# A hybrid attention block on one core: the top-k bisection's small instructions and passes, the compression's place in the attention units, and the order of the first step

## The reference, cut to what matters

```python
z = rmsnorm(h, norm_mix) @ w_in                 # one projection, split by columns
# NSA: compressed keys/values, selected blocks, sliding window
blocks = blocks + pos_emb                       # windows of 32 tokens, stride 16
kc = gelu(flat @ w1) @ w2                       # compress_tokens, for k and for v
# DSA: an indexer picks 256 keys for each query
score = einsum('bqh,bqhs->bqs', iw_c, relu(idx_logits))
score = where(key_pos <= t_c, score, NEG_INF)
_, sel = top_k(score, 256)                      # then softmax attention over those keys
y = sigmoid(g_A) * y_A + sigmoid(g_B) * y_B     # merged, projected, then a SwiGLU FFN
```

## Time and profile before

| what | value |
|---|---|
| median of 3 runs | 1703.89 us (1701.45 to 1705.29) |
| profiled execution | 1705.37 us, its span 1703.7 us |
| PE busy | 1611.9 us (95%) |
| DVE busy | 1236.4 us (73%) |
| ACT / POOL busy | 689.7 / 617.8 us (40% / 36%) |
| mean granted clock | 0.987 |

### The profile page before, as it was taken

One profiled execution on the slowest core, in us unless ns is written; L12 is line 12 of the kernel. 1 busy time (PEld: TensorE's weight loads), 2 busy tenths in 40 slices (PEclk: granted clock), 3 DMA queues, 4 the chain that ended last, 5 costly groups with the idle time before them and its releaser, 6 DMA issues.

```text
span 1703.7 us, 25436 instructions
## 1 busy us (share of the span) xinstructions
PE 1611.9 (95%) x9216; PEld 1356.0 (80%) x9216; DVE 1236.4 (73%) x2208; ACT 689.7 (40%) x1383; POOL 617.8 (36%) x440
## 2 busy tenths in 40 slices
PE   5899979999989988999999988999999999999997
PEld 5777777888868877789878877888888888887885
DVE  5778897999944756788776328676776667668978
ACT  5554343321155657666622023423222222343445
POOL 3224223322141124434322024444444443544454
PEclk9999999999999999999999999999999999999999
DMA  5013132633161201001034441234333224374433
GB/s 192 13 50 113 58 101 80 191 99 99 50 161 50 101 26 51 14 14 39 26 124 149 130 142 62 62 105 126 101 116 110 93 93 161 132 268 158 153 112 117
DMA packets 153691, 172.19 MB, mean 101 GB/s; under 512 B 19552, under 2 KB 103520, under 8 KB 153312
## 3 DMA queue, kind: packets, MB, share of 16 engines
q1 hardware_dynamic: 153568, 170.57, 31.5%
HBM read 121.00 MB, written 49.55 MB: 100 GB/s over the span
## 4 chain that ended last, share of the span: by engine, by line
PE 48%; DMA 3%; DVE 3%; issue 1%; POOL 1%; ACT 1%; SPq 0%; DVEq 0%; ACTq 0%
PE psA L1554 9%; PE psA L1556 9%; PE psA L1555 8%; PE psT L1555 5%; PE psT L1556 5%; PE psT L1554 5%; PE psT L1561 2%; DMA wd<-in_w_down_dram 2%; PE psT L1757 2%; PE psA L1646 1%; PE psA L1647 1%; POOL w_lo L396 1%; DVE h L2343 0%; DMA gates<-scratch_gates 0%; DVE h L2359 0%
## 5 line engine op out<-in xcount | busy, mean ns | idle before, releaser
L396 POOL TENSOR_TENSOR w_lo<-w_raw,w_hi 128x1024 fp32r<-128x1024 f32 (+2 forms) x52 | 120.4, 2319 | 249.0 <-ACT w_hi L391 249.0
L1377 ACT ACTIVATE s<-s,nmax 128x640 f32<-128x640 f32 (+7 forms) x192 | 144.0, 752 | 37.7 <-DVE nmax L2214 36.3
L1154 POOL TENSOR_TENSOR w_lo<-w_sum,w_hi 128x1024 fp32r<-128x1024 f32 x44 | 115.6, 2629 | 119.8 <-ACT w_hi L1440 119.8
L1177 POOL TENSOR_TENSOR w_lo<-act_raw,w_hi 128x512 fp32r<-128x512 f32 x77 | 106.9, 1390 | 108.7 <-ACT w_hi L1468 108.7
L1561 PE MATMUL psT<-ident,s 128*128 128x128 f32 x816 | 120.9, 278 | 1.6 <-ACT pT L1387 1.6
L1554 PE MATMUL psA<-w_hi,xTh 128*128 128x512 f32 (+2 forms) x320 | 121.4, 379 | 0.2 <-issue 0.2
L1556 PE MATMUL psA<-w_hi,xTl 128*128 128x512 f32 (+2 forms) x320 | 118.4, 370 | 0.0
L1555 PE MATMUL psA<-w_lo,xTh 128*128 128x512 f32 (+2 forms) x320 | 118.3, 370 | 0.0
L1561 PEld LDWEIGHTS psT<-ident,s 128*128 128x128 f32 x816 | 95.1, 142 | 17.2 <-issue 7.1
L2434 DVE TENSOR_TENSOR w_lo<-wd,w_hi 128x512 fp32r<-128x512 f32 x77 | 89.3, 1163 | 23.8 <-ACT w_hi L1475 23.3
L2303 DVE COPY pT<-psT 128x512 f32<-128x512 f32 (+1 forms) x116 | 69.7, 600 | 49.8 <-PE psT L1561 49.7
(11 more groups left out here) (371 smaller groups left out, 4780.4 us busy)
## 6 DMA issues: line engine op xcount, KB each, us to landing
act_raw<-scratch_act SPq DMA_DIRECT2D x77, 256.0 KB, 3.0
w_raw<-in_w_in_dram SPq DMA_DIRECT2D x28, 512.0 KB, 4.1
scratch_act<-act SPq DMA_DIRECT2D x33, 256.0 KB, 2.1
scratch_act<-act_sum SPq DMA_DIRECT2D x33, 256.0 KB, 2.1
wd<-in_w_down_dram SPq DMA_DIRECT2D x33, 256.0 KB, 3.0
scratch_gates<-gate_out SPq DMA_DIRECT2D x32, 256.0 KB, 2.9
gates<-scratch_gates SPq DMA_DIRECT2D x32, 256.0 KB, 4.3
a<-in_w_gate_dram SPq DMA_DIRECT2D x22, 256.0 KB, 3.2
```

The lines of the kernel that those rows point to most:

```text
L396: nc.gpsimd.tensor_tensor(self.lo[n % RING][:, 0:u], self.raw[n % RAW][:, 0:u], self.hi[n % RING][:, 0:u].bitcast(F32), ALU.subtract).then ...
L1154: nc.gpsimd.tensor_tensor(lo2[n % RING][:], block_of(n)[:], hi2[n % RING][:].bitcast(F32), ALU.subtract)\
L1177: nc.gpsimd.tensor_tensor(lo2[slot][:, 0:512], act_raw[n % 6][:], hi2[slot][:, 0:512].bitcast(F32), ALU.subtract)\
L1377: a_.activation(s_sb[v % SR][:, 0:n], s_sb[v % SR][:, 0:n], ACT.Exp, scale=-1.0, bias=nmax[:, BR[a], i, h:h + 1], accum_out=psum_p[:, BR[a ...
```

## The change

The diff has four parts.

1. **Bisection.** `bit_cur` is no longer kept. `bit_try` carries the trial from bit to bit: `bit_keep` becomes the bit where the count was too small, and one scalar_tensor_tensor takes it out of the trial and puts the next bit in. So a bit has two small instructions, and the memset and the last exclusive-or go.
2. **Passes.** IN_STEP for WKV is 1; the last tile's step of a group (i = 7) gets 2 passes; the step behind the first pair (i = 1) gets BEHIND_PAIR: 3, 6, 1, 4. A group has 13, 24, 7, 14 passes, 58 in all, and 134 are left for the end.
3. **Compression.** X_AT becomes 11, 19, 27, 35, each one unit behind a tile's row factors on POOL; CH_AT 43, CK_AT 46, so the kT loads are issued with k = 6, behind the queries of tile 6 and ahead of those of tile 7.
4. **First step.** SP issues weight chunk 0 ahead of the gain row and chunk 1 ahead of x tile 1. ACT roots one column of the identity first, and squares tile 1 after `x_hi(0)`. PE runs `z_step(0)` directly behind `x_turn(0)`, with `x_turn(1)` inside it after two of its four chunks.

```diff
-    CH_AT, CK_AT = 36, 38
-    X_AT, MASKS_AT = [10, 17, 23, 28], 44
+    CH_AT, CK_AT = 43, 46
+    X_AT, MASKS_AT = [11, 19, 27, 35], 44
...
         load_x(0)
+        w1.load(sp, 0)
         sp.dma_start(gain1[:], A["norm_mix"][0:1, :].to_broadcast([P, D])).then_inc(gain_in, 16)
-        w1.load(sp, 0)
+        w1.load(sp, 1)
         load_x(1)
-        w1.load(sp, 1)
         load_x(2)
...
+        act.wait_ge(consts, 2)
+        a_.activation(stat[:, 2, 0:1], ident[:, 0:1], ACT.Sqrt)
         x_square(0)
         x_root(0)
-        x_square(1)
         for n in range(2):
             w1.split_hi(act, n)
         for k in range(NT + 3):
             if k < NT:
                 x_hi(k)
+            if k == 0:
+                x_square(1)
...
-        def z_step(q):
+        def z_step(q, between=None):
...
             for a in range(KT // 2):
                 n = 4 * (q // NT) + a
+                if between is not None and a == 2:
+                    between()
...
         for k in range(NT + 3):
-            if k < NT:
+            if k < NT and k != 1:
                 x_turn(k)
-            if 0 <= k - 1 < NT:
+            if k == 0:
+                z_step(0, lambda: x_turn(1))
+            if 1 <= k - 1 < NT:
                 z_step(k - 1)
...
         def sign_bound():
-            v_.memset(bit_cur[:], 0)
             then(v_.tensor_scalar(bit_flip[:, R], count[:, R], float(TOPK), -1.0, ALU.is_lt, ALU.mult))
+            then(v_.tensor_scalar(bit_try[:, R], bit_flip[:, R], 1 << 30, None, ALU.bitwise_xor))

         def bit_bound(bit):
-            then(v_.tensor_scalar(bit_keep[:, R], count[:, R], float(TOPK), float(1 << bit), ALU.is_ge, ALU.mult))
-            then(v_.tensor_tensor(bit_cur[:, R], bit_cur[:, R], bit_keep[:, R], ALU.bitwise_or))
+            then(v_.tensor_scalar(bit_keep[:, R], count[:, R], float(TOPK), float(1 << bit), ALU.is_lt, ALU.mult))
+            then(v_.scalar_tensor_tensor(out=bit_try[:, R], in0=bit_keep[:, R], scalar=(1 << bit) >> 1, in1=bit_try[:, R],
+                                         op0=ALU.bitwise_or, op1=ALU.bitwise_xor))
...
-            elif k == 0 and bit < 31:
-                then(v_.tensor_scalar(bit_try[:, R], bit_cur[:, R], 1 << bit, None, ALU.bitwise_or))
-                then(v_.tensor_tensor(bit_try[:, R], bit_try[:, R], bit_flip[:, R], ALU.bitwise_xor))
...
-            then(v_.tensor_tensor(bit_try[:, R], bit_cur[:, R], bit_flip[:, R], ALU.bitwise_xor))
...
-        PASSES, IN_STEP = 32 * NTK, {QB: 2, CMP: 4, WKV: 2, QA: 2}
+        PASSES, IN_STEP, BEHIND_PAIR = 32 * NTK, {QB: 2, CMP: 4, WKV: 1, QA: 2}, {QB: 3, CMP: 6, WKV: 1, QA: 4}
...
-                some_counts((2 if q - 1 in PAIRED else 1) * IN_STEP[zsteps[q][0]])
+                c, i = zsteps[q]
+                some_counts(BEHIND_PAIR[c] if i == 1 else 2 if i == NT - 1 else IN_STEP[c])
```

## The result

The changed kernel takes 1688.1 us (median; 1684.4 to 1688.6), the kernel before 1703.9 on the same chip: ratio 0.989, 95% interval 0.987 to 0.991. The forecast was 1688.2. Its profiled execution spans 1686.9 us against 1703.7. The total is right, in part by luck. Of its terms one was wrong and another was right for a reason that was partly wrong, and only the experiments and the rows behind them showed that.

What follows compares the result with a forecast made beforehand. PE, busy 1611.9 of 1703.7 us, was taken as the bound, so only its idle or lower-clock time could be won. Gains 2.9 + 7.0 + 3.7 + 2.1 = 15.7 gave 1688.2 against the median, range 1683 to 1697.

Steps and rivals of the forecast that it cites:

- Start: First step: chunk 3 lands sooner, so `z_step(0)` ends near 23.5 and `x_turn(2)` follows earlier; 2.9 us gained, bounds 1.3 to 3.5.
- Rival B: Start: the new order gives nothing, PE held by tile 1 or the gain row; time about 1692, chance 0.12.
- Stage 2: Turn behind the first WKV pair: PE's wait shrinks from 7.26 to about 2.1; with clock 7.0 us gained, bounds 4 and 9.
- The clock's 1.8: Behind stage 2's long wait: the 3.12 us at clock 0.50 go, adding 1.8 us to the gain.
- L: End of the bisection: lateness of `selection` against PE, 10.5 later with 7.86 in hand, so 2.6 us.
- The page that spoke against the new instruction: Bisection's end: port rule would hold about six new bit ends for 1.2 each; L 2.1, time 0.5 lower.
- Front: First attention units: copy goes ahead of the windows, so POOL no longer holds PE's row-factor turn; 3.7 us gained.
- Clock behind the turn: Behind the row-factor turn's wait: the 3.20 us at clock 0.50 go; 2.1 us gained.
- A: Gate stage and first scores: selection holds PE longer; with three more holds L is 8, time 1693.6; chance 0.18.
- D: Stage 2 and front: change doesn't reach PE, something else late ends the 7.26 wait; within 3 us of 1704; chance 0.02.
- C: `bit_bound`: scalar_tensor_tensor takes 1.87 each time, L is 41.7 and the kernel slower at 1727; chance 0.04.
- The signs: Right: `x_turn(2)` at 23 to 24, bits of 5.73, no `row_factors_wide` wait; wrong: bits over 5.9, waits for q or kT.

Runs made afterwards that it cites:

- second profile: The changed kernel unaltered, run once more beside the variant with two further moves: 1691.4 us, ratio 0.990 to the kernel before.
- old last passes: Changed kernel with the old number of passes (4, 8, 4 or 4) behind each group's last step instead of 2: 1696.4 us, ratio 0.993.
- the start alone: Kernel before with only the new order at the start: 1702.7 us, ratio 0.998.
- two small instructions alone: Kernel before with only the shorter bit update, two small instructions instead of four: 1703.9 us, ratio 0.999.
- passes alone: Kernel before with only the new numbers of counting passes per step, still four small instructions a bit: 1709.0 us, ratio 1.002.

## Why the prediction was right, point by point

- **Start, 2.9 predicted, 2.8 measured, for a reason partly wrong.** What bounds the new step was right: chunk 3's load behind the low part of chunk 1, the last low part predicted to end at 22.2, measured 22.4 (22.44, where PE's last wait ends, is that moment). But it came only 0.8 earlier than before. The other 2.0 is PE's new order, which the prediction has in one clause ("which no longer stand behind each other"). Rival B's argument that chunk 3 was last before is wrong: PE came to it 2.1 late. One step failed, "Now chunks 0 and 1 come before the gain and tile 1": the loads' order is worth 0.2 to 0.4. What makes chunk 1's low part early (it ended at 13.5, predicted near 12.5, before 16.1) is that tile 1's square left its place ahead of the casts, an edit that I had booked only as a delay. Tile 0 was turned not 0.4 earlier but 0.4 later: its scaling began at 8.32 and took 1.85 instead of 1.28, held by the low part of chunk 0 that POOL now had under way (7.01 to 9.09). That cost nothing, since the step's end hangs on the chunks.
- **Stage 2, 7.0 predicted, 7.3 measured, 6.2 in the second profile.** The wait shrank by 5.3 against 5.2 predicted. The old last passes bring it back, as the experiment shows. The clock's 1.8 came in most profiles and not in all: behind the wait of 1.96 it stayed at 1.00 in eight of the nine profiles that have that wait, and fell in the changed kernel's second; behind the five waits of 6.2 to 8.2 it fell every time.
- **L, 2.6 predicted, 0.1 measured: the failed term.** "Net, `selection` ends 10.5 later against PE" was 7.9 (from 7.27 ahead of the first score to 0.63 behind it). The bit's length (5.73) was exact. The step that failed is that I had left the holds as they were. Behind 290 us the kernel before had five small instructions over 0.4, 6.8 us beyond their 0.2, and the changed one two, 4.3: 2.5 saved. One more, in `selection` itself (2.53 at 436.65, before only), saves 2.1, as what stood behind it waited too. One new hold takes 1.7 back: with two passes ahead of it instead of four, the low part of block 39 now runs into one of POOL's (300.00 to 302.40), and takes 2.36 instead of 0.69 (DVE, changed kernel):

```profile
300.59 2.36 DVE L2050 TENSOR_TENSOR blocks<-roped,blocks 128x512 fp32r<-128x512 f32 x1
```

So 10.5 - 2.5 - 2.1 + 1.7 = 7.6, near the 7.9.

- **The page that spoke against the new instruction.** The Trainium skill (SBUF — State Buffer, Who interferes with whom) was read as making about half of twelve new bit ends held. The scalar_tensor_tensor can be held (2.24 at 403.02 in the variant without the compression move), so the rule's mechanism stands; the count does not follow from a share of POOL's time but from the beat above. The same section says that the tensor_scalar form that also writes its accumulator is not among those that take the shared pair, and these traces agree: a 768-element counting pass that began inside a low part (325.64, the low part from 325.06 to 327.46, the start alone) took 1.01, as it does elsewhere.
- **Front, 3.7 predicted, 4.7 measured.** It is 6.33 - L minus what POOL still holds. With L gone PE came early enough to meet POOL's wait for the tables; I had put the copy at 488.09 and, 10 us earlier as all of it is, it came at 478.45, but did not count that PE could arrive before it.
- **Clock behind the turn, 2.1 predicted.** From this turn to the second tile's it took 8.2 us instead of 9.9, 1.7 less, and to the end of the span 2.0 less. The second figure is no proof: the changed kernel's second profile took 3.1 longer for that long stretch than its first (1210.9 against 1207.8).
- **Rivals.** A is the mechanism that decides: without the cheaper bit it makes the change a loss (16.2 us of wait), with six passes more it costs 6 of the 16 us won. Its place was exactly right, and for this edit it did not come. B falls with the start alone, D with the single parts, C with 0.17 us for the instruction.
- **The signs.** `x_turn(2)` came at 24.55 and not at 23 to 24: behind the step PE waited for tile 2's scaling. The turn behind the pair waited 1.96, at full clock in one profile of two. PE's 2 to 3 of idle before the first unit did not come (0.1), and a wait for `row_factors_wide` stayed (1.59). In the first profile PE also waited 0.41 for the queries at 489.71, in the second not. Of the signs of a wrong forecast that 0.41 is the only one: bits stayed at 5.73 and the clock of the second tile's first units at 1.00.
- The errors were of opposite sign: L 2.5 too high against PE's gain, then 1.6 of wait that nobody had booked. By the two profiled spans 16.8 was won, 1.1 more than the sum of 15.7. It is the medians that agree within 0.1 us, of executions that lie 4 us apart, so that closeness is luck.

## What to carry to other kernels

An edit that thins filler work where the critical engine waits is only half an edit: the filler goes to the end of its queue, and the slack there decides. Measure that slack first (here the first unit's idle row, 7.86 us), and buy what is missing by a cheaper unit of filler. And when one engine's periodic small instructions can be held by another's periodic long ones, count the holds by the beat of the two periods, with the shift that each hold itself brings, not by the share of busy time; a few per cent of a period's length change the number by a factor of two.

## What the runs showed of the hardware that was not expected

- Holds of 128x6 tensor_scalar and scalar_tensor_tensor instructions, 0.17 us otherwise, last until POOL's low part ends (2.42 for the one that began with a low part of 2.40, at 404.72), and come once per beat: every 32.5, 43.5 and 65.1 us for bits of 6.14, 5.93 and 5.73 us.
- The granted clock falls to 0.50 (1.2 GHz) without a long wait. Behind the same 2.5-us wait (208.55 before, about 205 in the variants) the clock stood at 0.50 for 3 to 4 us in five of fourteen profiles (the kernel before, two small instructions alone, passes alone, and both profiles of the changed kernel) and at 1.00 in nine. Where it stayed up, the first score came at 467.5 to 468.4 in the five profiles of variants that share the changed kernel's work up to there; in the changed kernel's own two profiles, where it fell, at 469.45 and 470.42 (in the second it fell again behind the wait of 1.96). So single profiles differ by 2 to 3 us in a stretch in which the same instructions run, as much as the smallest terms of the prediction.
- Behind the wait of 16.2 us PE worked on at 0.50 for nearly 6 us, as against 3 to 4 behind the 7.3 of the earlier trace rows. The wait's length alone does not set it: behind the 6.23 of the old last passes (219.79) it was nearly 6 us too.
- The root's table load costs 1.28 us at 0.80, in ACT's idle start, and the root that had followed it at 5.89 takes 0.20 with no further pause.
